# Group norm on eight rows, the gate and bonus moved forward, the state's decay on VectorE, samples' outputs from the old state

## What is computed

```python
def step(S, inp):
    r_t, w_t, k_t, v_t, kk_t, b_t = inp
    S_kk = jnp.einsum('bhvk,bhk->bhv', S, kk_t)
    S = S * w_t[:, :, None, :] - S_kk[..., None] * b_t[:, :, None, :] + v_t[..., None] * k_t[:, :, None, :]
    return S, jnp.einsum('bhvk,bhk->bhv', S, r_t)
...
g = jax.nn.sigmoid(gd) @ g_up
...
mean = jnp.mean(o, axis=-1, keepdims=True)
var = jnp.mean(jnp.square(o - mean), axis=-1, keepdims=True)
o = ((o - mean) * lax.rsqrt(var + GN_EPS)).reshape(B, T, W) * gn_w + gn_b
bonus = jnp.sum(r_h * k_h * r_k, axis=-1, keepdims=True) * v_h
out = (o + bonus.reshape(B, T, W)) * g
...
x = x + jnp.concatenate([o_rwkv, o_mla], axis=-1) @ w_out[l]
```

## Time and profile before

| | |
|---|---|
| time, median of 3 (lowest, highest) | 1905.67 us (1904.67, 1909.27) |
| the profiled execution's own time | 1913.24 us |
| its span | 1911.7 us |
| mean granted TensorE clock, share of full speed | 0.971 |
| TensorE matmul busy | 1788.4 us (94%) |
| VectorE busy | 638.0 us (33%) |
| ScalarE busy | 315.1 us (16%) |
| GpSimd busy | 84.5 us (4%) |
| DMA, mean over the span | 153 GB/s, 291.58 MB |

### The profile page before, as it was taken

How to read it: one execution, slowest core, us unless ns; L and a number is a source line. 1 busy time by engine, 2 the same in 40 slices (tenths; PEclk the granted TensorE clock), 3 DMA queues, 4 the chain that set the end, 5 groups by cost and what they waited for, 6 DMA issues and landing times.

```text
span 1911.7 us, 30695 instructions
## 1 busy us (share of the span) xinstructions
PE 1788.4 (94%) x11846; PEld 1483.9 (78%) x11846; DVE 638.0 (33%) x1250; ACT 315.1 (16%) x617; POOL 84.5 (4%) x99
## 2 busy tenths in 40 slices
PE   6999999878889999999999999997798999999995
PEld 5888887558767888888888888874686878888884
DVE  3111136548563321111121112546585612311122
ACT  1111002432100311110011100134221013111100
POOL 0000000014000000000000000000320000000000
PEclk9999999989899999999999999999799999999998
DMA  5444543841246634443434455346303474344431
GB/s 202 146 141 176 196 165 109 221 136 47 103 169 218 219 137 160 143 154 146 162 133 138 147 205 201 127 143 188 117 27 138 172 272 150 130 137 151 170 125 78
DMA packets 70641, 291.58 MB, mean 153 GB/s; under 512 B 8209, under 2 KB 41170, under 8 KB 41730
## 3 DMA queue, kind: packets, MB, share of 16 engines
q1 hardware_dynamic: 63938, 246.57, 37.7%
q0 software_dynamic: 6448, 42.20, 6.0%
q10 hardware_dynamic: 144, 1.32, 0.2%
HBM read 281.47 MB, written 8.59 MB: 152 GB/s over the span
## 4 chain that ended last, share of the span: by engine, by line
PE 86%; DVE 9%; ACT 2%; issue 2%; DMA 1%; DVEq 0%; SPq 0%; POOL 0%; ACTq 0%; POOLq 0%
PE bank L366 81%; DVE arena L1450 3%; PE bank L878 3%; PE bank L369 2%; ACT arena L1206 1%; DVE ring_a L1450 1%; DVE arena L1487 1%; DVE arena L1465 1%; DMA ring_c<-in_blocks 1%; DVE hT L1459 0%; DVE arena L1462 0%; DVE sq L1450 0%; DVE sq L1621 0%; DVE hT L1450 0%; DVE arena L1454 0%
## 5 line engine op out<-in xcount | busy, mean ns | idle before, releaser
L366 PE MATMUL bank<-hT,ring_a 128*128 128x264 f32 x2816 | 629.5, 387 | 18.9 <-DVEq L97 18.7
L366 PEld LDWEIGHTS bank<-hT,ring_a 128*128 128x128 f32 x2816 | 535.9, 190 | 111.1 <-issue 19.3
L366 PE MATMUL bank<-arena,ring_b 128*128 128x264 f32 x1408 | 314.3, 386 | 5.1 <-DVE arena L1514 5.1
L366 PEld LDWEIGHTS bank<-arena,ring_b 128*128 128x128 f32 x1408 | 267.2, 190 | 52.3 <-issue 6.8
L366 PE MATMUL bank<-arena 64*64 64x64 f32 (+6 forms) x3568 | 190.4, 273 | 20.8 <-DVE arena L1450 11.8
L366 PE MATMUL bank<-hT,ring_c 128*128 128x264 f32 x832 | 195.4, 393 | 12.5 <-DVE hT L1450 5.8
L366 PEld LDWEIGHTS bank<-hT,ring_c 128*128 128x128 f32 x832 | 158.8, 193 | 46.9 <-issue 8.4
L366 PEld LDWEIGHTS bank<-arena 64*64 64x64 f32 (+3 forms) x3568 | 149.1, 135 | 55.2 <-issue 44.4
L366 PE MATMUL bank<-arena,ring_c 128*128 128x264 f32 (+1 forms) x768 | 174.0, 385 | 1.3 <-ACT arena L1206 1.3
L366 PEld LDWEIGHTS bank<-arena,ring_c 128*128 128x128 f32 x768 | 144.9, 190 | 28.5 <-issue 5.0
L1206 ACT ACTIVATE arena<-bank 128x512 f32<-128x512 f32 (+5 forms) x220 | 95.4, 434 | 304.8 <-PE bank L366 255.6
(11 more groups left out here) (143 smaller groups left out, 1084.5 us busy)
## 6 DMA issues: line engine op xcount, KB each, us to landing
ring_a<-in_ffn_gu SPq DMA_DIRECT2D x88, 1024.0 KB, 4.8
ring_c<-in_blocks SPq DMA_DIRECT2D x58, 1024.0 KB, 4.9
ring_b<-in_ffn_down SPq DMA_DIRECT2D x32, 1408.0 KB, 6.2
arena<-in_pages SPq DMA_DIRECT2D x128, 144.0 KB, 2.5
arena<-in_mem_k POOLq DMA_DIRECT2D x8, 1024.0 KB, 7.8
arena<-in_mem_v POOLq DMA_DIRECT2D x8, 1024.0 KB, 7.2
ring_c<-in_pages SPq DMA_DIRECT2D x48, 144.0 KB, 2.5
ring_a<-in_pages SPq DMA_DIRECT2D x48, 144.0 KB, 2.4
```

Source lines behind the costliest of these rows:

```text
L366: return nc.tensor.matmul(out, lhsT, rhs, start=start, stop=stop)
```

## The change

- **Group norm.** A new constant `cen` (identity less 1/64 in a head's block) makes the centred value in one product; `sum8` sums a head's squares onto one of 8 rows; factor, epsilon, reciprocal and square root work on 8 rows; `bc8` spreads the result back to 128 rows. It is done twice: for the first 192 columns (`EARLY`) inside chunk 3, and for the last 72. The centred value times the gate stands in `oT` before the factor comes.
- **Gate and bonus.** The gate's products take the place of `keep_warm(4, 6)` in the attention; the bonus's product r, k, `r_k` stands behind the samples' attention on VectorE; its sums over heads are taken in `between(4)` and `between(5)`, and VectorE's `bonuses(4)` and `bonuses(5)` finish both (bonus plus bias times gate; gate times weight).
- **Decay.** `Zd = Z[n] * dcm[n]` on VectorE and a last addition take the place of the identity products. The `keep_warm(2)` of each chunk and of the norm go. TensorE's order in a chunk is u, new keys, state, outputs of the same chunk; before it was u, new keys, identity, outputs of the chunk before, state.
- **Samples.** Their outputs are made from the old state with two dot products (`s_dot`), in steps 2 and 3 of the levels. Five steps that make the new state follow: step 4 ahead of the output projection's loop on VectorE, 5 to 8 behind its tiles 1, 3, 5, 7.
- **Transfers.** SP loads `mem_k` 0 and 1 only. Pool's order becomes: sample outputs, prompt's state, `mem_k` 4 to 7, `mem`, samples' state, `mem_k` 2 and 3, `mem_v`.
- **Output projection.** TensorE waits for `z_out(4)` before half 0 of n = 2, and for the first or second `rwkv_mixed` (of two) before half 0 of n = 3 and the halves 1.

```diff
-                     ("keep", SEQ)):
+                     ("keep", SEQ), ("cen", P), ("sum8", NJ * H), ("bc8", NJ * P)):
...
+EARLY = 3 * CHUNK
...
+        squared = Bt.rearrange("p j t -> p (j t)")
+        Zd = G[0]
...
+        gate, bonus = w1, small[:, 0:NJ * NT].rearrange("p (j t) -> p j t", j=NJ)
+        r8 = wstat[0:H, :]
...
 if n == C_OUT + 1:
-    for b in range(4):
-        if b == 0:
-            sp.wait_ge(*signal("operands_ready").at(2))
-        if b == 2:
-            sp.wait_ge(*signal("so_ready").at(1))
-            sp.wait_ge(*signal("stored").at(4))
+    sp.wait_ge(*signal("operands_ready").at(2))
+    for b in range(2):
         signal(f"mem_k_loaded{b}").by(
...
-wait_apart(pool, signal("state_ready").at(1))
-stored.by(pool.dma_start(t["o_wkv_s"][layer], S.rearrange("p a b -> p (a b)")))
 wait_apart(pool, signal("so_ready").at(1))
...
 wait_apart(pool, signal("z_out").at(4))
 stored.by(pool.dma_start(t["o_wkv"][layer], Z[4].rearrange("p (j v) -> p j v", j=NJ)))
-wait_apart(pool, stored.at(5))
+wait_apart(pool, stored.at(4))
...
 wait_apart(pool, signal("rwkv_ready").at(4))
 for b in range(4, NS):
...
+    load_keys(b)
+wait_apart(pool, signal("rwkv_mixed").at(2))
 signal("mem_loaded").by(pool.dma_start(memg, t["mem"]))
+wait_apart(pool, signal("state_ready").at(1))
+stored.by(pool.dma_start(t["o_wkv_s"][layer], S.rearrange("p a b -> p (a b)")))
+wait_apart(pool, stored.at(5))
+for b in (2, 3):
+    load_keys(b)
...
 pe.wait_ge(*signal("sample_out").at(1))
+pe.wait_ge(*signal("gate_out").at(1))
...
-keep_warm(4, 6)
+pe.wait_ge(*signal("prob_t_out").at(units))
+pe.wait_ge(*signal("olat_out").at(units))
+pe.wait_ge(*signal("gd_ready").at(1))
+for j in range(NJ):
+    last = mm(bank[2 * j + 1 if j < 3 else 6][:, 0:NT], sw("g_up")[:, j * P:j * P + P], p[:, 13, :])
+signal("gate_up").by(last)
 wait_apart(pe, signal("s_weights").at(1))
...
 def between(n):
+    if n >= 4:
+        wait_apart(pe, signal("rkr_ready").at(1))
+        for i in range(2):
+            if n == 5:
+                wait_apart(pe, signal("bonus_out").at(i + 1))
+            else:
+                wait_apart(pe, signal("tok_out").at(9 + i))
+            signal("bonus_ready").by(mm(bank[6 + i][:, 0:NT], c("blk"), bonus[:, 2 * (n - 4) + i, :]))
...
+def centred(late):
+    n = columns(late)
+    width = n.stop - n.start
+    for j in range(NJ):
+        b, at = (3, j * width) if late else (j // 2, j % 2 * width)
+        last = mm(bank[b][:, at:at + width], c("cen"), oT[:, j, n])
+    signal("gn_centred").by(last)
+def variance(late):
+    n = columns(late)
+    width = n.stop - n.start
+    wait_apart(pe, signal("gn_squared").at(2 if late else 1))
+    sums = c("sum8", NJ)
+    for j in range(NJ):
+        last = mm(bank[0 if late else 2][0:H, 0:width], sums[:, j, :],
+                  squared[:, j * width:j * width + width], j == 0, j == NJ - 1)
+    signal("gn_variance").by(last)
+def spread(late):
+    n = columns(late)
+    width = n.stop - n.start
+    wait_apart(pe, signal("gn_rooted").at(2 if late else 1))
+    back = c("bc8", NJ)
+    for j in range(NJ):
+        b, at = (1, j * width) if late else ((2, 7)[j // 2], j % 2 * width)
+        last = mm(bank[b][:, at:at + width], back[0:H, j, :], r8[:, n])
+    signal("gn_spread").by(last)
...
 for n in range(4):
     T, cc = n // 2, n % 2
-    z = bank[6]
     if n:
-        keep_warm(2)
         wait_apart(pe, signal("z_out").at(n))
...
-    if n:
-        for j in range(NJ):
-            js = slice(j * P, j * P + P)
-            add(z[:, js], ident, Z[n][:, js])
-        outputs(n - 1)
-    wait_apart(pe, signal("u_out").at(n + 1))
...
+    else:
+        wait_apart(pe, signal("bonus_out").at(4))
+    if n < 3:
+        new_keys(n)
+        wait_apart(pe, signal("u_out").at(n + 1))
+        state(n)
+        if n == 0:
+            wait_apart(pe, signal("wt_out").at(2))
+        outputs(n)
+wait_apart(pe, signal("rwkv_out").at(3))
+centred(False)
+wait_apart(pe, signal("so_loaded").at(1))
+for j in range(NJ):
+    last = tp(bank[7][:, j * NS:j * NS + NS], so_tok[0:NS, j * P:j * P + P], NS)
+signal("so_turned").by(last)
+wait_apart(pe, signal("u_out").at(4))
 outputs(3)
+variance(False)
+wait_apart(pe, signal("rwkv_out").at(4))
+wait_apart(pe, signal("so_out").at(1))
+centred(True)
+new_keys(3)
+wait_apart(pe, signal("gn_scaled").at(1))
+variance(True)
+state(3)
+spread(False)
+spread(True)
...
-        if half:
-            pe.wait_ge(*signal("rwkv_mixed").at(j + 1))
+        if half and j == 0:
+            pe.wait_ge(*signal("rwkv_mixed").at(2))
...
-pe.wait_ge(*signal("gate_out").at(1))
 for n in range(4):
+    if n == 2:
+        pe.wait_ge(*signal("z_out").at(4))
+    if n == 3:
+        pe.wait_ge(*signal("rwkv_mixed").at(1))
     half(n, 0)
...
+act.wait_ge(*signal("gate_up").at(1))
+for j in range(NJ):
+    run(gate[:, j, :], bank[2 * j + 1 if j < 3 else 6][:, 0:NT], done="gate_out" if j == NJ - 1 else None)
...
+run(spare[:, 0:1], spare[:, 0:1], ACT.Sqrt)
...
+    if n == 2:
+        act.wait_ge(*signal("gn_centred").at(1))
+        for i in range(2):
+            run(squared[:, 2 * EARLY * i:2 * EARLY * i + 2 * EARLY], bank[i][:, 0:2 * EARLY], ACT.Square,
+                "gn_squared" if i else None)
+late = NJ * (NT - EARLY)
+act.wait_ge(*signal("gn_centred").at(2))
+act.wait_ge(*signal("gn_variance").at(1))
+run(squared[:, 0:late], bank[3][:, 0:late], ACT.Square, "gn_squared")
+for n, cols in enumerate((slice(0, EARLY), slice(EARLY, NT))):
+    act.wait_ge(*signal("gn_inverse").at(n + 1))
+    run(r8[:, cols], r8[:, cols], ACT.Sqrt, "gn_rooted")
...
+dve.wait_ge(*signal("pv_ready").at(NS))
+tt(flat(bonus), flat(rr), flat(kc), ALU.mult)
+for j in range(NJ):
+    ts(bonus[:, j, :], bonus[:, j, :], v("r_k", j), ALU.mult, done="rkr_ready" if j == NJ - 1 else None)
...
 if s == 2:
+    tt(svb[:, 3, :], svb[:, 1, :], svb[:, 0, :], ALU.mult)
+    tt(St, S, by_key(3), ALU.mult)
+if s == 3:
+    total(so, St)
+    for i, n in enumerate((4, 2)):
+        tt(svb[:, 5, :], svb[:, n, :], svb[:, 0, :], ALU.mult)
+        total(s_dot[:, i:i + 1], svb[:, 5, :])
+    stt(so, skk, s_dot[:, 0:1], so, ALU.mult, ALU.subtract)
+    stt(so, svv, s_dot[:, 1:2], so, ALU.mult, ALU.subtract, "so_ready")
+if s == 4:
     tt(S, S, by_key(1), ALU.mult)
-if s == 3:
+if s == 5:
     tt(St, last_dim(skk, *full), by_key(4), ALU.mult)
-if s == 4:
+if s == 6:
     tt(S, S, St, ALU.subtract)
-if s == 5:
+if s == 7:
     tt(St, last_dim(svv, *full), by_key(2), ALU.mult)
-if s == 6:
+if s == 8:
     tt(S, S, St, ALU.add, "state_ready")
-if s == 7:
-    tt(St, S, by_key(0), ALU.mult)
-if s == 8:
-    total(so, St, "so_ready")
...
+def group_norm():
+    early, late = slice(0, EARLY), slice(EARLY, NT)
+    dve.wait_ge(*signal("so_turned").at(1))
+    copy(oT[:, :, SEQ:NT], bank[7][:, 0:NJ * NS].rearrange("p (a b) -> p a b", a=NJ), "so_out")
+    for i in range(2):
+        js = slice(2 * i, 2 * i + 2)
+        dve.wait_ge(*signal("gn_squared").at(1))
+        tt(oT[:, js, early], bank[i][:, 0:2 * EARLY].rearrange("p (j t) -> p j t", j=2), gate[:, js, early],
+           ALU.mult, "gn_scaled" if i else None)
+    dve.wait_ge(*signal("gn_variance").at(1))
+    ts(r8[:, early], bank[2][0:H, 0:EARLY], 1.0 / HD, ALU.mult, GN_EPS, ALU.add)
+    chain(nc.vector.reciprocal(r8[:, early], r8[:, early]), signal("gn_inverse"))
+    dve.wait_ge(*signal("gn_squared").at(2))
+    tt(oT[:, :, late], bank[3][:, 0:NJ * (NT - EARLY)].rearrange("p (j t) -> p j t", j=NJ), gate[:, :, late],
+       ALU.mult)
+    dve.wait_ge(*signal("gn_variance").at(2))
+    ts(r8[:, late], bank[0][0:H, 0:NT - EARLY], 1.0 / HD, ALU.mult, GN_EPS, ALU.add)
+    chain(nc.vector.reciprocal(r8[:, late], r8[:, late]), signal("gn_inverse"))
+def bonuses(n):
+    if n == 4:
+        dve.wait_ge(*signal("gate_out").at(1))
+    for j in range(2 * (n - 4), 2 * (n - 4) + 2):
+        dve.wait_ge(*signal("bonus_ready").at(j + 1))
+        tt(bonus[:, j, :], bank[6 + j % 2][:, 0:NT], vv[:, j, :], ALU.mult, "bonus_out")
+        stt(bonus[:, j, :], bonus[:, j, :], v("gn_b", j), gate[:, j, :], ALU.add, ALU.mult)
+        ts(gate[:, j, :], gate[:, j, :], v("gn_w", j), ALU.mult)
...
-step_samples(n - 1)
+if n < 5:
+    step_samples(n - 1)
 if n < 5:
     at = CHUNK * n - 1
     tt(dcm[n - 1], over(c("blk"), P, NJ, P), din[:, :, at:at + 1].broadcast_to([P, NJ, P]), ALU.mult)
+if n >= 4:
+    bonuses(n)
...
     copy(U[T][rows, :], bank[3 * T][rows, 0:512], "u_out")
-    if n < 2:
-        step_samples(5 + 2 * n)
-        step_samples(6 + 2 * n)
+    if n:
+        tt(Zd, Z[n], flat(dcm[n]), ALU.mult)
+    if n == 3:
+        group_norm()
     dve.wait_ge(*signal("z_ready").at(n + 1))
...
+    tt(Z[n + 1], bank[6][:, 0:512], flat(dcm[n]), ALU.mult, None if n else "z_out")
+    if n:
+        tt(Z[n + 1], Z[n + 1], Zd, ALU.add, "z_out")
...
+    dve.wait_ge(*signal("gn_spread").at(1))
+    tt(oT[:, js, early], oT[:, js, early],
```

(18 more changed lines are left out.)

123 lines of the change are left out of this document (34 added, 89 removed).

## The result

| | before | changed |
|---|---|---|
| median, 8 runs each | 1905.17 us | 1891.54 us (1884.5 to 1896.19) |
| ratio, with its 95% interval | | 0.9931 (0.9902 to 0.996) |
| profiled execution, time and span | 1913.24, 1911.7 | 1895.58, 1894.0 |

The changed kernel is faster by 13.6 us (0.7%), where 34 were forecast. Beside later experiments it was measured twice more: 1896.72 against 1902.26 (0.9958, 0.9931 to 0.9985) and 1894.84 against 1900.2 (0.9958, 0.9924 to 0.9992). Its 32 executions lie between 1881.6 and 1906.6, those of before between 1892.5 and 1914.3, so no single execution tells much. The time goes with the mean granted clock: of the 87 executions of the kernel before that stand beside the experiments, those at 0.981 or more took 1892.5 to 1896.8, those at 0.972 or less 1911.4 to 1914.3, and the one profiled took 1913.24 at 0.971. The profiles tell where the time is.

A forecast was written before the change was run, and what follows sets the result against it. It took TensorE as the bound (86% of the chain), with VectorE stretches; tile 4 18.2 us earlier less 0.5 made 17.7 a layer, 35.4 in two, from 1905.7 to 1870.3, said as 1871; range 1858 to 1898.

The forecast's parts named there:

- theory E: Chunks, from the experiments: a step without a 128x264 product can fall to half clock and stay; with one it does not.

The follow-up runs named there:

- spread bonus: Changed kernel with the bonus's sums over heads and VectorE's triples spread over the last levels and chunk steps; 1876.32 against 1896.72 us.
- before_cold: Kernel before without the two unread products at the head of each chunk step and of the norm; 1928.82 against 1902.35 us.
- paced and filled forms: Changed kernel with `mem` and `mem_k` loads issued later (1890.33; thinner 1884.38), ten unread products in TensorE's bonus wait (1889.96), or thin loads plus those products (1876.11 us).
- spread kernels: Changed kernel with bonus sums and triples spread (1876.32), plus later loads (1873.6), or thinner loads (1868.37), or those and six unread products (1866.31, again 1866.53 us).
- one_wide: Changed kernel with thinly spread loads, ten unread products in the bonus wait and one unread 128x264 product in chunk steps 1 to 3; 1873.43 us.
- warm: Changed kernel with two unread 128x264 products put back at the head of chunk steps 1 to 3; median 1893.93 us.

## What to carry over

When a change brings a stretch forward, list every transfer that its new place puts in flight beside the next load that TensorE waits for, in MB over the rate of a full window (403 to 426 GB/s from 1450 to 1466 in the changed kernel), and put the load that is waited for first. Products that nothing reads may be holding the clock: take them out one at a time, and look at the granted clock of the stretch behind each. A step can go into an engine's wait inside a chain, as the spread bonus did. Before you subtract from a baseline, compare the granted clock of its profile with that of its other executions.

## What was not expected of the hardware

TensorE stood at 0.50 for 22 us while busy in every microsecond (changed kernel, layer 1), and for 41 in before_cold, busy 38.6 of 41.5. Whether the chunks fall differs between layers and executions of one program: of the 14 layers in the seven profiles of the changed kernel and of its paced and filled forms, ten had their chunks at full clock and four at half, 13.7 against 23 us for the same records. With one 128x264 product in a chunk step the profiled chunks had full clock in all 12 layers (the spread kernels, one_wide), with two it came back within a step (warm). Twelve of 12 against ten of 14 is too little to show theory E. What decides within one program stays open.
